# Turning the next head pair's queries and keys at the head of an attention turn instead of at its end

## The reference

```python
for l in range(DEPTH):                       # DEPTH = 2
    # l = 0: grouped-query attention (8 query heads, 2 key heads, 64 wide) || mLSTM (4 heads)
    # l = 1: neighbourhood attention (16 heads, 64 wide) with a bias per relative offset
    x = x + g1 * mixer(rms_norm(x, g_mix) * (1 + sc1) + sh1)
    x = x + g2 * hier_moe(rms_norm(x, g_ffn) * (1 + sc2) + sh2)

def attention(q, k, v):                      # per head
    s = q @ k.T * scale                      # layer 1: + bias inside the window, -inf outside it
    return softmax(s) @ v
```

## Time and profile before

| | |
|---|---|
| time, median of 3 runs | 1696.42 us (1694.55 to 1701.11) |
| the profiled execution | 1696.42 us, span 1694.5 us |
| mean granted clock of TensorE | 0.945 |
| busy: TensorE / VectorE / ScalarE / GpSimd | 90% / 27% / 18% / 9% |
| chain that ended last | TensorE 85%, VectorE 9%, DMA 2% |
| attention of layer 0 | about 264 to 316 us |
| attention of layer 1 | about 1028 to 1105 us |

### The profile page before, as it was taken

One profiled execution on the slowest core, in us unless ns is written; L12 is line 12 of the kernel. 1 busy time (PEld: TensorE's weight loads), 2 busy tenths in 40 slices (PEclk: granted clock), 3 DMA queues, 4 the chain that ended last, 5 costly groups with the idle time before them and its releaser, 6 DMA issues.

```text
span 1694.5 us, 21412 instructions
## 1 busy us (share of the span) xinstructions
PE 1525.0 (90%) x8379; PEld 717.5 (42%) x8379; DVE 454.5 (27%) x1067; ACT 301.9 (18%) x614; POOL 145.8 (9%) x200
## 2 busy tenths in 40 slices
PE   5999777878999999999948998886999999999991
PEld 4546765443433333333314444544433333333330
DVE  0013575534111111111122024833311111111113
ACT  3100205311111111111121003611111111111112
POOL 1012111100000000000005000010000000000000
PEclk9999887988999999999988998997999999999996
DMA  9989952235999999999969422023799999999982
GB/s 349 335 315 203 383 185 102 80 126 205 422 427 429 428 428 428 428 427 428 427 255 309 148 99 87 2 79 136 312 427 428 428 428 426 429 428 428 427 367 115
DMA packets 82919, 521.62 MB, mean 308 GB/s; under 512 B 10131, under 2 KB 11611, under 8 KB 56241
## 3 DMA queue, kind: packets, MB, share of 16 engines
q1 hardware_dynamic: 69536, 485.58, 70.1%
q0 software_dynamic: 13328, 35.29, 6.8%
HBM read 511.08 MB, written 20.22 MB: 314 GB/s over the span
## 4 chain that ended last, share of the span: by engine, by line
PE 85%; DVE 9%; DMA 2%; ACT 1%; issue 1%; POOL 1%; DVEq 0%; POOLq 0%
PE psum L840 25%; PE psum L853 14%; PE psum L528 13%; PE psum L821 10%; PE psum L786 5%; PE psum L846 3%; PE psum L833 2%; PE psum L452 2%; PE psum L827 2%; PE psum L494 1%; PE psum L701 1%; PE psum L714 1%; DVE area_q L1248 1%; DVE area_m L1248 1%; DVE small L1258 1%
## 5 line engine op out<-in xcount | busy, mean ns | idle before, releaser
L840 PE MATMUL psum<-ring,area_t 128*64 128x512 f32 x1024 | 449.9, 592 | 1.8 <-issue 0.9
L841 PE MATMUL psum<-ring,area_t 128*64 128x512 f32 x1024 | 450.0, 592 | 0.0
L840 PEld LDWEIGHTS psum<-ring,area_t 128*64 128x64 f32 x1024 | 140.1, 137 | 291.9 <-issue 291.9
L853 PE MATMUL psum<-ring,area_t 128*64 128x512 f32 x1024 | 233.8, 598 | 2.2 <-DVE area_t L1751 2.2
L528 PE MATMUL psum<-ring,area_t 128*128 128x512 f32 (+1 forms) x528 | 220.1, 578 | 0.0
L1722 DVE COPY area_q<-psum 64x512 f32<-64x512 f32 x64 | 44.4, 694 | 567.3 <-PE psum L841 567.2
L821 PE MATMUL psum<-area_h,area_t 128*64 128x512 f32 x768 | 181.0, 607 | 3.0 <-DVE area_t L1736 3.0
L528 PEld LDWEIGHTS psum<-ring,area_t 128*128 128x128 f32 x528 | 100.5, 191 | 116.2 <-issue 114.4
L1933 POOL DMA_INDIRECT pair_rows<-area_q,idx x64 | 62.4, 975 | 930.8 <-ACT area_q L1163 930.8
L841 PEld LDWEIGHTS psum<-ring,area_t 128*64 128x64 f32 x1024 | 140.1, 137 | 0.0
L853 PEld LDWEIGHTS psum<-ring,area_t 128*64 128x64 f32 x1024 | 68.5, 136 | 122.0 <-issue 122.0
(11 more groups left out here) (251 smaller groups left out, 1344.6 us busy)
## 6 DMA issues: line engine op xcount, KB each, us to landing
ring<-in_moe_w SPq DMA_DIRECT2D x192, 2048.0 KB, 14.7
ring<-in_ada_w SPq DMA_DIRECT2D x24, 2048.0 KB, 20.1
ring<-in_na_w_in SPq DMA_DIRECT2D x6, 2048.0 KB, 17.3
ring<-in_ab_w_in SPq DMA_DIRECT2D x5, 2048.0 KB, 18.5
area_m<-mod_ready POOLq DMA_DIRECT2D x6, 1024.0 KB, 9.5
area_q<-pair_rows POOLq DMA_DIRECT2D x6, 1024.0 KB, 7.3
ring<-in_ab_w_out SPq DMA_DIRECT2D x2, 2048.0 KB, 19.4
area_g<-mod_ready POOLq DMA_DIRECT2D x4, 1024.0 KB, 8.4
```

Source lines behind the costliest of these rows:

```text
L840: pe.matmul(banks[2 + u][0:64, :], lhsT, w1[:, k, :], start=(k == 0), stop=(k == KT - 1))
L841: mm = pe.matmul(banks[2 + u][64:128, :], lhsT, w3[:, k, :], start=(k == 0), stop=(k == KT - 1))
L853: mm = pe.matmul(banks[6 + u][64 * j:64 * j + 64, :], hidT[u][:, k, :], w2[:, k, 512 * j:512 * j + 512], start=(k == 0), stop=(k == 3))
```

## The change

TensorE does TQ(j+1) and TK(j+1) first in their turns, ahead of S, T and V. VectorE does CK(j+1) ahead of H instead of behind it. ScalarE's order is not touched, and no instruction, buffer or semaphore is added or taken away.

```diff
@@ attention(l) of TensorE @@
                 for i in range(NU[l] + 3):
+                    if i % NT == 0 and i // NT + 1 < NP[l]:
+                        turn_queries(l, i // NT + 1)
+                    if i % NT == 1 and i // NT + 1 < NP[l]:
+                        turn_keys(l, i // NT + 1)
                     if i < NU[l]:
                         scores(l, i)
                     if 2 <= i < NU[l] + 2:
                         turn_probs(l, i - 2)
                     if i >= 3:
                         values(l, i - 3)
-                    if i % NT == 0 and i // NT + 1 < NP[l]:
-                        turn_queries(l, i // NT + 1)
-                    if i % NT == 1 and i // NT + 1 < NP[l]:
-                        turn_keys(l, i // NT + 1)
                     if l == 0 and BOUT_AT <= i < BOUT_AT + NT:
                         turn_mixed_b(i - BOUT_AT)
@@ attention(l) of VectorE @@
                         normalise(i - 1)
+                    if i % NT == 1 and i // NT + 1 < NP[l]:
+                        copy_keys(i // NT + 1)
                     if i >= 3:
                         take_heads(i - 3)
-                    if i % NT == 1 and i // NT + 1 < NP[l]:
-                        copy_keys(i // NT + 1)
```

## The result

The changed kernel is slower: 1724.33 us (median; 1723.1 to 1727.08) against 1698.41, a ratio of 1.015 with a 95% interval of 1.0127 to 1.0174. Two more comparisons of the same kernel gave 1.0129 (1.0106 to 1.0152) and 1.0146 (1.0128 to 1.0164). By these ratios it is 22 to 26 us more, where 17.0 was forecast; 1724.33 lies in the range of 1705 to 1726, near its upper end.

The account below looks back on a forecast made before the run. The two attention stages were taken as bound by hand-overs between TensorE, VectorE and ScalarE. Layer 1's 11.9 us and layer 0's 5.1 gave 17.0 on 1696.42, so 1713.4 us; range 1705 to 1726.

Parts of the forecast that it names:

- The wait for the query copy: Both attention stages: key transposes, now first, wait for ScalarE's query copy and hold the scores; 1.55 us a steady pair.
- TQ off the path, 0.71 a pair: Steady pairs: query transposes fit into TensorE's 1.04 us idle time; gain 0.71 us, seven times in layer 1, three in layer 0.
- CK ahead of H is nothing: VectorE in both attention stages: swapping the copies of keys and heads costs nothing.
- The clock: Layer 1's steady pairs: TensorE keeps full clock despite 1.6 us idle; otherwise 1.86 us more for each of five pairs.
- a sign of being wrong: Layer 1: a granted clock falling below 0.9 would show the forecast wrong.
- The rival with the clock: Both attention stages: same waits with TensorE at the lower clock; 28.0 us more, 1724, up to 1730; chance 0.17.
- The forecast's own bounds: Whole kernel: 15.9 to 18.7 us slower, somewhat more for pairs whose clock rises late; 1711 to 1718 us.
- Layer 1, opening: Layer 1's first pair: the second unit's first VectorE work after its scores starts 2.9 us late, at the lower clock.
- The term "+11.9" for layer 1: Layer 1's attention: 2.9 us in the opening, 1.2 in the second pair, 7.8 in five more; the eighth has none.
- five times 1.55: Layer 1's five pairs after the second: 1.55 us more each, together 7.8 us.
- Layer 0: Layer 0's attention: VectorE's extra work covers part; three turns lose 2.4, 0.4 and 2.3 us, together 5.1.
- Nothing behind the stages absorbs it: After attention: output projection starts right after, its weights landed long ago; none of the 17.0 us is recovered.

Follow-up runs that it names:

- experiment 1: The kernel before with only the key transposes moved to the head of TensorE's turn: ratio 1.013, 1719.8 us against 1698.37.
- experiment 4: The changed kernel with ScalarE also copying the queries first in its turn: ratio 0.9996 against the kernel before.
- Experiment 2: The kernel before with only the query transposes moved to the head of TensorE's turn: ratio 0.9962, 6 us faster.
- experiment 3: The kernel before with only VectorE's copy of the keys moved ahead of its copy of the heads: ratio 1.0002.
- The fillings: The changed kernel with the middle unit's score matmuls repeated, unread, ahead of the key transposes: ratio 1.0105 once, 1.0087 twice, beside 1.0146 without; an earlier single filling 1.0115.
- experiment 7: The kernel before with the whole change in layer 1 alone, layer 0 keeping its old order: ratio 1.0099, 17 us slower.

## Why the prediction was right or wrong

**The wait for the query copy: right.** The chain from T to F was put at 4.39 us and measured 4.40, piece by piece as worked out (0.91, 0.70, 0.69, 0.50, 0.06, 0.58, 0.96). The idle time before TK was put at 1.6 and is 1.61. The pair was put at 10.03 and is 9.96. Experiments 1 and 4 show the cause from both sides: TK's move alone gives a loss of that size, and an earlier copy takes all of it back.

**TQ off the path, 0.71 a pair: right.** Experiment 2's pair is 7.77, which is 8.48 - 0.71. The gain of the stage was larger than that, 8.2 us in layer 1 instead of 5: the opening took 12.5 us from the first key copy to the third in place of 17.0 (1040.27 less 1035.52, then 7.71; before 6.25 and 10.73), and the stage's granted clock rose from 0.93 to 1.00. Part of that may be spread between profiles: in experiment 3, with TensorE's old order, the same stretch took 14.6 us. The step left out what the clock can give, here and in what follows.

**CK ahead of H is nothing: right** in time (experiment 3; and the full-clock pair of experiment 1, without this move, is 9.96 us as in the changed kernel). It isn't quite nothing in the trace: V of the last unit now waits 0.49 us until H has freed its bank, which is why TensorE stands only 0.28 before T and not the 0.8 that I gave. (The bracket names ScalarE's copy of another unit, which ends at 1096.19; by the kernel's code this V waits for H, which ends at 1096.13.) T was not late by it.

**The clock: the step that failed.** I took the full clock for every steady pair, since 1.6 us lay nearer to the 1.40 of the earlier trace rows than to the 2.43 of the earlier trace rows, and so put the clock at nothing for them in the sum. In the changed kernel four of layer 1's intervals from key copy to key copy are 11.2 to 11.6 us, and the stage's granted clock is 0.85. That is below the 0.9 which I had named as a sign of being wrong. The fillings put the clock's share at about 10 us of the 25. The rival with the clock had 28.0 us, and at 22 to 26 the result lies between it and the forecast: some pairs fell and some did not, which neither case had. The forecast's own bounds ended at 1718; that 1724.33 is inside the range is owed to the part of it that stood for the clock.

The length of one idle time was the wrong thing to read: 1.61 us came before pairs at either clock. How much of the loop TensorE is idle doesn't tell it either. That went up from 1.04 of 8.48 us to 2.38 of 9.96, and filling it made every steady pair run at full clock. But in experiment 1 TensorE was idle for 9.82 of 39.86 us, as large a part, and those pairs all kept the clock. So idle time in the pairs is part of the cause, and what picks the pairs that fall stays open.

By the Trainium skill ("TensorE: Matmul & The Clock Gate", HAM oscillation — how this bites in real kernels), the clock can fall again and again when a wait follows each burst of matmuls; its example has waits for DMA of some 3 to 5 us. The trace agrees with the repeated fall (granted clock 1.00, then 0.75), and not with such lengths: in those two pieces TensorE never stood idle for more than 1.61 us.

**Layer 1, opening: mis-sized.** F(1) was to come 2.9 us late on the assumption of the lower clock. In the changed kernel's profiles this part ran at full clock, and the interval between the first two key copies grew only from 6.25 to 7.44, by 1.2. The term "+11.9" for layer 1 measured 14.3: 1.2 in the opening, 0.9 in the second pair (1.2 foreseen), then +2.9, +1.5, +1.5, +2.7, +3.1 where five times 1.55 stood, and 0.7 behind the last.

**Layer 0: the mechanism right, the size short.** E(6) to F(7) was put at 3.99 and is 3.98 (302.27 to 306.25). But TK of the second pair ran at the lower clock, the case for which I had +2.1 instead of +0.4, and H of that pair then waited 0.80 for V, which I hadn't counted. H of the third pair still waited 0.87, where I had its idle time used up. From key copy to key copy the three pairs grew by 2.9, 1.5 and 2.9 where 2.4, 0.4 and 2.3 stood, and 1.0 came behind them. The stage grew by 8.3 in the first profile where 5.1 stood; against old-order profiles of 48.8 to 52.1 us the three profiles of the change have 56.8 to 60.4.

**Nothing behind the stages absorbs it: right.** The stages' growth of 22.6 us and the measured 22 to 26 agree.

## What to carry to other kernels

An instruction that waits should stand behind work that doesn't: before moving it to the head of a turn, add up the chain that releases it on the other engine, every instruction ahead of it there included, and compare with the time at which the queue reaches it. Two moves in one edit can have opposite signs: here the query transposes alone gain 6 us and the key transposes alone lose 21, and the whole is not their sum. When a wait thins out TensorE's work, price it twice, once as time and once for the granted clock; and let the range hold both, since here neither the longest hole nor the idle part of the loop told which pairs would fall.

## What the runs showed of the hardware

Two matmuls without use, put into each of ten waits (1.35 to 3.97 us long in the first profile of the change), made the kernel 7 us faster, and four of them 10 us (ratios 1.0146, 1.0105, 1.0087). The same hole of 1.61 us came before groups of score matmuls that took 0.92 and 1.65 us in one stage, so it is not the single hole that decides. The same pairs were hit in three profiles of one kernel, and others in experiment 7, whose order in that layer is the same. In experiment 1 a loop as idle as this one ran four pairs in a row at a granted clock of 1.00. Which rule does decide was not measured.
